# Modulation vectors of a hybrid decoder layer: two ahead of the chunks, four in blocks during them

## The reference, cut to what matters

```
mod = c @ w_ada + b_ada                          # (9, 1024) @ (1024, 6144)
sh1, sc1, g1, sh2, sc2, g2 = split(mod, 6)
u = x * (1 + sc1) + sh1
p, xr, gr = split(u @ w_in, 3)                   # w_in (1024, 1536)
y_pool = causal multi-scale pooling of p, then @ w_pool
xc = causal_conv(xr);  r, i = sigmoid(xc @ w_a), sigmoid(xc @ w_x)
h = linear recurrence with a(r), b(i, xc);  y_lru = h * gelu(gr)
x = LN(ALPHA * x + (1 + g1) * (concat(y_pool, y_lru) @ w_out))
y = mixture of 16 experts (top group, top 2) on x * (1 + sc2) + sh2
x = LN(ALPHA * x + (1 + g2) * y)
```

## Time and profile before

| | |
|---|---|
| median of 3 runs | 1362.23 us |
| the profiled execution's own time, and its span | 1362.96 us, 1361.2 us |
| first product of chunk 1 | 162.4 us into the span |
| from chunk 1 to chunk 2 and on to chunk 8 | 43.7 us each, chunk 8 starts at about 468.3 us |
| busy shares over the span | PE 91%, DVE 68%, ACT 37%, POOL 26% |
| DMA over the span | 231.36 MB, 170 GB/s |

### The profile page before, as it was taken

How to read it: one execution, slowest core, us unless ns; L and a number is a source line. 1 busy time by engine, 2 the same in 40 slices (tenths; PEclk the granted TensorE clock), 3 DMA queues, 4 the chain that set the end, 5 groups by cost and what they waited for, 6 DMA issues and landing times.

```text
span 1361.2 us, 23166 instructions
## 1 busy us (share of the span) xinstructions
PE 1240.9 (91%) x6695; PEld 977.1 (72%) x6696; DVE 928.6 (68%) x1827; ACT 503.2 (37%) x936; POOL 355.0 (26%) x439
## 2 busy tenths in 40 slices
PE   6796899999999997999999729999999999999596
PEld 1122599999999986888877528888888888888342
DVE  1105559888988898989899985565665556523188
ACT  1010444355444643211111024454654454422175
POOL 0004021122202243221211023343445445432100
PEclk9897899999999998999999859999999999999798
DMA  8992010222202435544343368777998888864673
GB/s 264 392 343 74 1 40 18 75 92 92 61 31 92 170 105 182 171 146 164 124 140 126 116 215 264 216 200 207 273 296 214 248 257 254 255 166 88 182 297 147
DMA packets 119241, 231.36 MB, mean 170 GB/s; under 512 B 11413, under 2 KB 70041, under 8 KB 119157
## 3 DMA queue, kind: packets, MB, share of 16 engines
q1 hardware_dynamic: 105375, 180.50, 38.6%
q0 software_dynamic: 13824, 50.34, 16.1%
HBM read 161.49 MB, written 69.97 MB: 170 GB/s over the span
## 4 chain that ended last, share of the span: by engine, by line
PE 66%; DVE 19%; issue 5%; ACT 4%; DMA 3%; SPq 1%; POOL 1%; DVEq 0%; ACTq 0%; POOLq 0%
PE bank L1536 17%; PE bank L1538 17%; PE bank L1537 17%; PE bank L1483 5%; PE bank L1510 5%; PE bank L1603 2%; DVE ada_arena L1464 1%; DVE arena L1183 1%; DMA arena<-in_w_in 1%; DVE arena L1057 1%; PE bank L1557 1%; DVE arena L1071 1%; PE bank L1674 1%; DVE ada_arena L1450 1%; DMA ada_arena<-in_w_ada 1%
## 5 line engine op out<-in xcount | busy, mean ns | idle before, releaser
L1536 PE MATMUL bank<-parts 128*128 128x256 f32 (+2 forms) x1472 | 512.1, 348 | 19.2 <-DVE parts L1380 9.8
L1538 PE MATMUL bank<-parts 128*128 128x256 f32 (+2 forms) x1472 | 496.8, 337 | 0.0
L1537 PE MATMUL bank<-parts 128*128 128x256 f32 (+2 forms) x1472 | 496.2, 337 | 0.0
L1536 PEld LDWEIGHTS bank<-parts 128*128 128x128 f32 x1472 | 282.5, 192 | 51.5 <-issue 13.9
L1538 PEld LDWEIGHTS bank<-parts 128*128 128x128 f32 x1472 | 282.2, 192 | 28.8
L1537 PEld LDWEIGHTS bank<-parts 128*128 128x128 f32 x1472 | 282.8, 192 | 25.9
L1483 PE MATMUL bank<-ident,arena 128*128 128x128 f32 (+4 forms) x788 | 116.9, 281 | 13.6 <-DMA arena<-u_d,tok_i 6.0
L1483 PEld LDWEIGHTS bank<-ident,arena 128*128 128x128 f32 (+4 forms) x788 | 94.1, 146 | 40.2 <-DVE parts L1048 7.7
L1373 DVE TENSOR_TENSOR parts<-arena,parts x90 | 104.9, 1221 | 14.8 <-ACT parts L885 14.3
L1385 DVE TENSOR_TENSOR arena<-arena,bank 128x256 f32<-128x256 f32 x48 | 20.2, 421 | 133.2 <-ACT arena L895 130.7
L1510 PE MATMUL bank<-ada_arena,cT 128*9 128x512 f32 x192 | 85.8, 609 | 15.8 <-DMA ada_arena<-in_w_ada 15.8
(11 more groups left out here) (254 smaller groups left out, 1856.9 us busy)
## 6 DMA issues: line engine op xcount, KB each, us to landing
ada_arena<-in_w_ada SPq DMA_DIRECT2D x12, 2048.0 KB, 11.7
arena<-in_w_gate SPq DMA_DIRECT2D x16, 1024.0 KB, 5.9
arena<-in_w_up SPq DMA_DIRECT2D x16, 1024.0 KB, 12.7
arena<-in_w_down SPq DMA_DIRECT2D x16, 1024.0 KB, 14.6
y_d<-zero SPq DMA_DIRECT2D x17, 512.0 KB, 6.2
arena<-in_x_prompt SPq DMA_DIRECT2D x8, 1024.0 KB, 7.0
yT_d<-arena SPq DMA_DIRECT2D x16, 512.0 KB, 4.6
arena<-yT_d SPq DMA_DIRECT2D x16, 512.0 KB, 6.1
```

The lines of the kernel that those rows point to most:

```text
L1536: pe.matmul(out, x_hi, w_hi, start=start, stop=False)
L1537: pe.matmul(out, x_hi, w_lo, start=False, stop=False)
L1538: return pe.matmul(out, x_lo, w_hi, start=False, stop=stop)
```

## The change

`w_ada` is read in three groups of 2048 columns (two modulation vectors each). Group 0 (sh1 and sc1) is loaded whole, in four pieces of two row blocks, and multiplied ahead of the chunks. The other two groups are multiplied one row block of 128 at a time while the chunks run: four blocks in chunk 1 (behind orders 5, 7, 9 and 11), two in each of chunks 2 to 7 (behind orders 1 and 2), each from one of two 1 MB buffers, loaded a chunk ahead. Banks 4 and 5 hold the sums of these groups over all chunks, so the gates move to banks 0, 1, 6 and 7. In all groups the four 512-column quarters of a row block go to the four 32-row strips of one bank, each a 128x32 tile of PE at another column position; the stationary operand is `cT` padded to 32 columns. POOL copies the row block of `cT` that the next chunk needs into `c_now`. `w_in` is loaded, split and used by column group and half (`IN_ORDER`); chunk 1's x is turned during the sample rows; the sample's gates and pooling move behind order 1 of chunk 1. After DVE's program of chunk 7 the two late sums are formed and stored, and SP has two of the loads of `w_out` behind that.

The diff, cut to its core:

```diff
-            with sp.Fori(1, 4) as j:
-                sp.wait_ge(S["w_in_in"], 16 * j)
-                sp.dma_start(w_in[:, ds(2 * j, 2), :], w_in_d[:, ds(2 * j, 2), :]).then_inc(S["w_in_in"], 16)
-                for n in range(3):
-                    sp.wait_ge(S["ada_mm"], 3 * j + n - 2)
-                    sp.dma_start(w_ada[n], ada_d[ds(3 * j + n, 1)].rearrange("a p k n -> p (a k) n")).then_inc(S[f"ada{n}"], 16)
+            for n in range(4):
+                sp.dma_start(w_ada0[:, 2 * n:2 * n + 2, :], ada_d[0][:, 2 * n:2 * n + 2, :]).then_inc(S[f"ada{n}"], 16)
...
+            sp.wait_ge(S["cT_mm"], 1)
             sp.dma_start(xin, xp_d[0]).then_inc(S["x_loaded"], 16)
+            for n, (q, h) in enumerate(IN_ORDER):
+                if n == 2:
+                    load_mixer_weights()
+                sp.dma_start(in_half(q, h), w_in_d[:, 4 * h:4 * h + 4, q, :]).then_inc(S[f"w_in{n}"], 16)
...
+            with sp.Fori(2, NCH - 1) as i:
                 load_x(i + 1)
+                sp.wait_ge(S["ada_mm"], 2 * i + 3)
+                load_ada(1, i + 1, 0)
+                load_ada(2, i + 1, 1)
                 store_y(i)
                 zero_tiles(i)
...
             load_x(NCH)
-            for k in (4, 5, 6):
+            zero_tiles(NCH - 1)
+            sp.wait_ge(S["ada_mm"], 2 * NCH + 1)
+            for k in (4, 5):
                 load_out(k, "w_out_in")
-            zero_tiles(NCH - 1)
             sp.wait_ge(S["y_stored"], 16 * TPC * (NCH - 2) + 16)
+            sp.wait_ge(S["late_ok"], 1)
+            for n in range(2):
+                for j in range(4):
+                    sp.dma_start(mod_rows[n + 1, j], mod_late[n][CW * j:CW * j + NM, :]).then_inc(S["mod_stored"], 16)
             sp.wait_ge(S["out_evac"], 3)
             load_out(7, "w_out_in")
+            sp.wait_ge(S["mod_stored"], 16 * 8)
+            load_out(6, "w_out_in")
...
+            uT_evac(1, range(KD // 2))
+            in_hi(0)
+            in_hi(1)
+            uT_evac(1, range(KD // 2, KD))
+            in_hi(2)
+            rows_evac(0)
+            in_hi(3)
+            in_hi(4)
+            rows_evac(1)
+            in_hi(5)
+            rows_evac(2)
...
+            def mod_sum(dst, src, n):
+                return dve.scalar_tensor_tensor(dst, src, one_a[:, n:n + 1], dst, ALU.add, ALU.add)
...
             o.leave(NCH - 1)
+            dve.wait_ge(S["bl_in"], 128)
+            dve.wait_ge(S["ada_mm"], 2 * NCH + 1)
+            for n in range(2):
+                o.did(mod_sum(mod_late[n], bank[4 + n][:, :], n + 1))
+            o.wait()
+            dve.memset(spare[0:1, 0:1], 0.0).then_inc(S["late_ok"], 1)
             chunk(NCH, last=True)
...
+            def ada(k, g, w, start, stop):
+                row = c_now[:] if k is None else cT[:, k, :]
+                for j in range(4):
+                    last = pe.matmul(bank[(2, 4, 5)[g]][CW * j:CW * j + CW, :], row, w[:, DH * j:DH * j + DH], start=start, stop=stop)
+                return last
...
+            def late_ada(i, order):
+                if isinstance(i, int) and i == 1:
+                    steps = {5: (0, 1, 0, 1), 7: (0, 2, 0, 2), 9: (1, 1, 0, 3), 11: (1, 2, 0, 4)}
+                else:
+                    k = KD - 1 if isinstance(i, int) else None
+                    steps = {1: (k, 1, 0, i + 3), 2: (k, 2, 1, i - 1)}
+                if order in steps:
+                    k, g, b, n = steps[order]
+                    pe.wait_ge(S[f"ada_in{b}"], 16 * n)
+                    if k is None:
+                        pe.wait_ge(S["c_now"], i - 1)
+                    ada(k, g, w_ada[b], k == 0, k == KD - 1).then_inc(S["ada_mm"], 1)
...
+            turn_chunk(1, range(KD // 2), first=True)
+            pe.wait_ge(S["uTs_ready"], 1)
+            sample_rows(0)
+            turn_chunk(1, range(KD // 2, KD), first=True)
+            sample_rows(1)
+            turn_rows(0)
+            sample_rows(2)
+            turn_rows(1)
+            turn_rows(2)
...
+            mixers(1, lambda: turn_chunk(2), sample=sample_mixers)
+            with pe.Fori(2, NCH - 1) as i:
                 mixers(i, lambda: turn_chunk(i + 1))
+            mixers(NCH - 1, lambda: turn_chunk(NCH))
```

More of the change, by code:

```diff
@@ L160, in build @@
         row_d, row_e = at(18600, DH), at(18056, DH)
-        w_ada = [place(ada_arena, 10240 + n * 4096, KD, 512) for n in range(3)]
-        mod = place(ada_arena, 22528, 6 * D)
+        w_ada0 = ada_at(0, KD, ADA)
+        w_ada = [at(2048, ADA), at(5184, ADA)]
+        mod0 = ada_at(24576, DH)
+        mod_late = [at(8768 + n * DH, DH) for n in range(2)]
         c_rows = at(0, D)
@@ L232, in build @@
         ones = sb("ones", [P, P])
-        cT = sb("cT", [P, KD, NM])
+        cT = sb("cT", [P, KD + 1, CW])
+        one_a = sb("one_a", [P, 3])
+        c_now = sb("c_now", [P, CW])
         modT = sb("modT", [P, 2 * KD, NM])
@@ L701, in _, with in_hi, uT_evac @@
             o.did(act.activation(sp_t[:, 1, :], sp_t[:, 0, :], ACT.Exp, scale=-1.0))
[L704 to L712, removed]
+            def in_hi(n):
+                act.wait_ge(S[f"w_in{n}"], 16)
+                act.wait_ge(S["ada_mm"], 1)
+                act.activation(half(w_in_hi, *IN_ORDER[n]), in_half(*IN_ORDER[n]), ACT.Copy).then_inc(S["win_hi"], 1)
+            def uT_evac(i, rows=range(KD)):
+                for k in rows:
                     act.wait_ge(S["xT_ready"], KD * (i - 1) + k + 1)
@@ L996, in _ @@
                     o.did(dve.memset(inv_cnt[:, g, t:t + 1], 1.0 / min(w, t + 1)))
[L998 to L1009, removed]
+            o.did(dve.memset(one_a[:], 0.0))
+            o.wait()
+            o.did(dve.memset(one_a[64:P, 0:1], 1.0))
+            o.did(dve.memset(one_a[0:64, 1:2], 1.0))
+            o.did(dve.memset(one_a[:, 2:3], 1.0))
             dve.wait_ge(S["st_mm"], 1)
@@ L1568, in column, with mixers @@
                 return NG + order if order < NG else order - NG if order < 2 * NG else order
-            def mixers(i, turn_next, states=None):
+            def late_ada(i, order):
[10 more added lines that the diff above has]
+                    ada(k, g, w_ada[b], k == 0, k == KD - 1).then_inc(S["ada_mm"], 1)
+            def mixers(i, turn_next, sample=None, states=None):
                 for order in range(3 * NG):
+                    if sample is not None and order == 2:
+                        sample()
                     if order == 2 * NG:
@@ L1584, in mixers, with turn_chunk @@
                     turn_next()
-            def turn_chunk(i, first=False):
+            def turn_chunk(i, rows=range(KD), first=False):
                 pe.wait_ge(S["x_loaded"], 16 * i)
-                for k in range(KD):
+                for k in rows:
                     if not (first and k < 4):
                         pe.wait_ge(S["uT_lo_ok"], KD * (i - 1) + k - 3)
-                    if k == 2:
+                    if k == 2 and not first:
                         pe.wait_ge(S["pool_evac"], NG * i)
```

188 lines of the change are left out of this document (108 added, 80 removed).

## The result

The changed kernel takes 1301.34 us (median of 4 runs, 1299.57 to 1304.18), the kernel before 1362.72 beside it (1362.06 to 1364.29): a ratio of 0.9548, interval 0.9529 to 0.9567. That is 61 us less, 18 us more than the forecast's 43 and inside the range.

A forecast was written before the change was run, and what follows sets the result against it. The head was taken as bound by DMA and PE, the chunks by PE alone. Terms: -97.4 + 34.3 + 3.0 + 1.0 + 5.5 + 10.4 = -43.2 us from 1362.96, forecast 1319, range 1295 to 1350.

The forecast's parts named there:

- The head: Before chunk 1: its first product starts at about 65 us instead of 162.4, a gain of 97.4 us.
- an overlap by one record: Products of a block: each overlaps its neighbour by one record, 2.14 us a block, 1.7 for a row block before chunk 1.
- The late blocks: Chunks 1 to 7: 16 blocks of four products cost PE 2.14 us each, 34.3 us in all.
- the broken pace: Chunks 1 to 7: every block breaks the column products' pace, 16 x 0.19 = 3.0 us.
- the next group's first record waits in line behind it: Within a block: a product's second record waits for its first and holds up the next group, giving 2.14 us a block.
- The second rival: Blocks: all four products run fully beside each other, 13.7 us in all, 20.6 less, time 1297 us; chance 0.22.
- the sum: Whole kernel: all terms together change the time by -43.2 us.
- Reloads: Chunk 1: one weight buffer is reloaded three times, about 1 us of waiting in all.
- The rival of late weights: Chunks 2 to 7: block weights come late; with 8 us of wait a chunk the time is 1367 us; chance 0.04.
- The sample's mixers: Chunk 1: PE's order 2 waits 5.5 us for the sample's guard, roots and order 0's evacuation.
- Chunk 8: Late sums, stores and w_out's last load delay ACT; PE stops about 17 us; cost 10.4 us, between 8 and 16.
- the forecast's own case: Whole kernel: the prediction's own partial overlap in the blocks, 1319 us, alone 1309 to 1330; chance 0.41.

The follow-up runs named there:

- The experiments with zeros: Changed kernel plus four products with zeros in each late block: spread over all four column groups 1316.12 us, all in one group 1358.91 us.
- all three repairs: Changed kernel with late sums in chunk 7, sample's mixers spread over chunk 1, and PE starting chunk 1 on 8 evacuations instead of 12: 1280.49 us.

## Why the prediction was right, step by step

- *The head* (-97.4): -99.1. The loads set when the vectors are ready, as the prediction had it, and the products ended at 32.8 (forecast 31.4). From there to chunk 1 it took 30.5 us instead of 33.6: the sample's rows 23.9 instead of 25.8 (36.91 to 60.81), the last step 2.5 instead of 3.7. That the last piece's products took about the forecast's time (3.64 us, forecast 3.4) is luck: the forecast had an overlap by one record at the full clock, and the runs have the full overlap at half the pace (last section).
- *The late blocks* (34.3 + 3.0 for the broken pace): mis-sized. The step "the next group's first record waits in line behind it" failed. A product's second record holds up only its own group: the four first records start together at 95.26, the four second ones at 95.71. So all four products run beside each other, 1.08 us a block up to the next column product, 17.3 for 16 (17.5 by the lengths of the chunks) instead of 37.3. The second rival had the mechanism: its 13.7 with the sum's 3.0 for the pace is 16.7. The experiments with zeros show it from both sides: 0.86 us for four products more in four groups, 3.41 in one. On the Trainium skill, "TensorE: Matmul & The Clock Gate", "Part 3: Packing small matmuls — row/col tiling": its 2.38 times is for three groups; taken for four, as in the prediction, it would make 1.44 us of a block. Here four groups take 1.06 instead of 3.43, 3.2 times, and the four products more cost a quarter of what they cost in one group, so the trace agrees that groups run concurrently. Its figure for three no run here tests. The drain between tiling modes (the Trainium skill, "TensorEngine Tiling (Array Packing)", "Tiling Modes") would have its place where the pace breaks: the block starts 0.21 us behind its neighbour instead of 0.12, and the second product behind it 0.23 behind the first instead of 0.12. That is 0.2 us a block, 3.2 for 16 (the 3.0 of the sum). Not all of it can be the column groups: with the sample's mixers spread, a group of float32 products of the full 128 columns starts 0.12 behind its neighbour (70.19 to 70.31), without a break, but behind it the second product follows at 0.20 too (71.12 to 71.32). So about 0.08 of the 0.2 is found without a change of tile too, and some 0.12 is left for the drain, if it is that.
- *Reloads* (1.0): none; no wait on a `w_ada` load in the chunks. The rival of late weights is out.
- *The sample's mixers* (5.5): 9.7, and 4.3 for a granted clock at its half level behind the gaps, which the sum didn't have at all. I carried over the guard's distance of 11.7 us from the last evacuation, as if DVE's chain still ran by itself. But its third difference waits for a pooling product, and the guard for tanh steps behind PE's gates, and PE now issues both behind orders 0 and 1. Spreading the mixers gave 8.5 back, which shows the size of the two terms together, not of each.
- *Chunk 8* (10.4): 10.9, by the chain forecast (ACT's split 38.2 us into chunk 8; PE's gap 18.0 instead of 17). Moving the sums took it all back.
- By the profiles the sum was 15.7 us too high: 19.8 from the blocks, 1.7 from the head, 1.0 from the reloads and 2.2 from the rest, less the 8.5 and 0.5 that the sample's mixers and chunk 8 cost more. By the medians it is 18, since the profiled execution of the changed kernel is itself 2.8 above its median (0.7 before).
- The direction and the range held, but not by the forecast's own case, which gave 1309 to 1330 alone. The time lies in the range because this was drawn out to the full overlap, and because two errors pulled against each other: without the 8.5 us that the sample's mixers cost beyond the sum it would be about 1293, below the range (an estimate).

## What to carry to other kernels

Here four float32 products with 32 output rows cost about a third of single file, because each writes a column group of its own in one bank: put such products together in one block, one to each group, and let the loads, not the products, decide where the block stands. Before work is moved from a stretch bound by two resources into one bound by PE, price the block both side by side and in single file (here 1.08 or 3.43 us, 16 times), and measure which it is. And look at what the moved work now waits for: what was early before (a sum ahead of a store ahead of a load, a small chain over three engines) comes late in its new place, and can be spread or drawn forward by a program of a few lines.

## What was not expected of the hardware

The 1.06 us of a block holds only at one pace. In the changed kernel's head two blocks took 3.64 us although the granted clock that the profile prints for these windows is 1.00; with all six vectors in the head the same two blocks took 1.92 us at a granted clock of 1.00 and 3.58 at 0.53 (PE windows of that run):

```profile
69.20:71.20 2.00, 1.92 (x16) 0.42 (x16) 0.00 (x0) 0.00 (x0) 0.00 (x0) 1.00 1.01 422
74.20:77.80 3.60, 3.58 (x16) 0.59 (x16) 0.00 (x0) 0.00 (x0) 0.00 (x0) 0.53 1.01 419
```

So 3.6 goes with the half level. The 1.00 beside the first pieces is no reading: the changed kernel's trace has intervals of the granted clock only from 38.6 us of the span on, and a window ahead of the first interval shows 1.00 for want of one. With all three repairs the first interval starts at 28.2, at the full level, and the pieces on either side of it are (PE):

```profile
23.80 3.64 PE L1589 MATMUL bank<-ada_arena,cT 128*32 128x512 f32 x16 [1.34 <-DMA ada_arena<-in_w_ada]
29.50 1.92 PE L1589 MATMUL bank<-ada_arena,cT 128*32 128x512 f32 x16 [2.06 <-DMA ada_arena<-in_w_ada]
```

In the other experiments the intervals start between 16.4 and 23.0 us, and it is the same there: a piece that ended before took 3.64 us, and one that lay wholly in an interval at the full level 1.92 or 1.93. So the first pieces ran at the half level, which is worked out from these times and not printed. It did cost time: the first three pieces were each done before the next had landed, but the sum waits for the end of the last. With all three repairs the last piece ended 1.4 us earlier than in the changed kernel (31.42 against 32.82), and chunk 1 began 1.6 earlier.
